# First norm scaled in the turn of the tokens, and its inputs loaded in another order

## The chip, the core and the metric

One core of a Trainium2 chip runs the whole kernel. The metric is device time in microseconds (us), lower is better. PE is TensorE, ACT ScalarE, DVE VectorE, POOL GpSimd, SP SyncE, which issues most of the DMA loads.

## What is computed

Two blocks one after the other on 256 tokens of 1024 channels in fp32. The change is in the first steps of the first block, for 16 meta tokens and the 256 of the input, T = 272 in all:

```python
h = jnp.concatenate([meta, x], axis=1)
u = rmsnorm(h, norm1_w[l])          # h * rsqrt(mean(h * h) + 1e-6) * norm1_w
proj = u @ w_in[l]
...
h = h + jnp.concatenate([out_a, out_b], axis=-1) @ w_out[l]
```

Behind it come the two mixers on `proj`, the output product, a gated MLP, and in the second block a modulation (`cond` times `w_ada`), retention, and a mixture of 16 experts whose weights (400 MB) are read from memory once.

## The kernel before

Every engine runs its own program, written out by hand; semaphores (`ev("name")`) order them. Activations lie with channels on the partitions: `hT` is the stream, `uT` the normed stream, each 8 tiles (KT) of 128 channels by 272 tokens. The inputs come with tokens on the partitions (`tok`, three windows of 128, 128 and 16 tokens), so they are turned first: PE's tile `x{k}` is made of three transposes (one a window, stationary operand a piece of `tok`, moving operand the identity), DVE copies it to `hT`. Tiles take turns in TB = 3 banks of PSUM in the order of the list `seq`; `open_tile` waits until the tile three before it is freed.

The start runs so. SP loads the constants `cst` (identity first, then masks and others, 1 MB), then the tokens in four loads; ACT issues ten small loads of parameter rows (`prow`, 124 rows). SP waits for all of these before it issues the first weights. PE waits for constants and tokens, turns x0 to x7 (L658), turns the parameter rows (L664, copied to `par` by DVE, L1587), and sums the squares with a matrix of 1/1024 (L649, tile n1); the squares are ACT's (L1274), written to `uT`. ACT takes the root of n1 (L1245), DVE its reciprocal over 128x272 (L1571), and scales each tile into `uT` (L1603): `hT` times norm1's weight times that reciprocal. PE's first projection tile p0 waits tile by tile for `uT` (`u_full`), and for its weights.

Weights stream through a ring of 2 MB units in the order of use (`stream(u)`, L502): u0 is the first block of `w_in`, for p0 to p3, u1 the first of `w_ada` (products L683, behind p3, which need `cond`), u2 the weights of p4 to p7, and so on. Behind u1 SP issues 20 more small loads (`more_parameters`), some of them of elements of 4 or 64 bytes. Projection tiles are L842, 8 products of 128x272 each; fp32 products are two instructions. ACT evicts tile p{j} (L1222); p0 to p11 feed DVE's convolution (`conv`, L1632, L1634), whose silu is ACT's (L1288). Other lines that are spoken of: L712 are transposes, L779 score products of 128x128, L1181 the experts' first products, L1093 later products of the second block.

Of the kernel before, what the change touches and what calls it, by code (L numbers as in the profile page):

```python
# [23 lines left out]
P = 128  # L24
D = 1024
# [123 lines left out]
def build(nc, a, out):  # L149
    with ExitStack() as ctx:  # L150
# [86 lines left out]
        chan = A.take(2, T)[0:16]  # L237

# [246 lines left out]
        def _(sp):  # L485
# [3 lines left out]
            load(cst[:], a["cst"], "cst_loaded")  # L489
# [107 lines left out]
        def _(pe):  # L597
# [213 lines left out]
            for j in range(NPROJ):  # L811
# [404 lines left out]
        def _(act):  # L1216
# [44 lines left out]
            rows("norm1", r1(a["norm1_w"]))  # L1261
            rows("lb0", r1(a["hg_lb_logits"][0:1]))
            rows("lb1", r1(a["hg_lb_logits"][1:2]))
            rows("hgn", r1(a["hg_norm_w"]))
            rows("m2cw", r1(a["m2_conv_w"][0]))
            rows("m2cb", r1(a["m2_conv_b"]))
            rows("m2n", r1(a["m2_norm_w"]))
            rows("norm2", r1(a["norm2_w"]))
# [6 lines left out]
            act.wait_ge(ev("par_ready"), 1)  # L1275
            act.wait_ge(ev("cond_cleared"), 1)
# [4 lines left out]
            act.wait_ge(ev("lb_shift"), 1)  # L1281
            act.activation(small[:, 0:16], small[:, 0:16], ACT.Exp).then_inc(ev("lb_exp"), 1)
            root("n1", T)
# [84 lines left out]
            for j in range(NPROJ):  # L1368
# [194 lines left out]
        def _(dve):  # L1563
# [16 lines left out]
            dve.memset(cond[:], 0.0).then_inc(ev("cond_cleared"), 1)  # L1580
            for k in range(KT):
                dve.wait_ge(ev("tiles_done"), k + 1)
                dve.tensor_copy(hT[:, k, :], bank_of(f"x{k}")[:, 0:T]).then_inc(ev("tiles_freed"), 1)
                dve.wait_ge(ev("tiles_freed"), k + 1)
                dve.nop().then_inc(ev("stream_tiles"), 1)
            dve.wait_ge(ev("par_turned"), 1)
            dve.tensor_copy(par[:, 0:PAR_ROWS[0]], ps[:, 3, 0:PAR_ROWS[0]]).then_inc(ev("par_ready"), 1)  # L1587
            dve.wait_ge(ev("par_ready"), 1)
# [4 lines left out]
            dve.nop().then_inc(ev("lb_shift"), 1)  # L1593
# [10 lines left out]

            inverse_root(T)
            for k in range(KT):
                scaled("norm1", k, 0)
# [16 lines left out]
            def conv(t):  # L1624
# [3 lines left out]
                if t == 0:  # L1628
                    dve.wait_ge(ev("tiles_done"), TN["n1"] + 1)
# [211 lines left out]
            for j in range(NPROJ):  # L1841
# [56 lines left out]
            for k in range(KT):  # L1898
                add_tile(f"o{k}", k, KEPT0)
                if 1 <= k < KT - 1:  # L1900
                    dve.wait_ge(ev("squares"), 2 * KT + k + 1)
# [325 lines left out]
```

## Time and profile before

| | |
|---|---|
| runs | 1725.61 us median of 3 (1721.76 to 1726.12) |
| the profiled execution | 1730.88 us, span 1729.1 us |
| PE busy | 1374.9 us, 80% of the span |
| DVE, ACT, POOL busy | 481.6, 409.9, 231.6 us |
| DMA | 523.98 MB, mean 303 GB/s; 430 GB/s in the second half |
| granted clock of PE, mean | 0.891 |
| chain that ended last | DMA 46%, PE 44%, DVE 7%, ACT 2% |

The profile is one execution with times from the span's start. Its rows name the engine, the line of the kernel, what is written and read, and how often. In groups the figures are busy us and mean ns of one instruction, then the engine's idle time before them and what ended it; in timelines and chains the start and the length in us; in windows of one engine the length, its busy time (instructions), the granted clock, the DMA share and GB/s. A granted clock of 1.00 is 2.4 GHz and 0.50 is 1.2 GHz.

### The profile page before, as it was taken

The numbers are of one execution on the slowest core, as the hardware profiler recorded it, in microseconds if no ns is written. First come the engines' busy times: TensorE is split into PE (matmuls) and PEld (weight loads), VectorE is DVE, ScalarE is ACT, GpSimd is POOL, SyncE is SP. The second block draws the span as 40 slices with busy tenths as digits, with TensorE's granted clock in tenths as the row PEclk, the third lists the DMA queues.
The fourth block names the chain that finished last, engine by engine and source line by source line (L and its number), as shares of the span: only waits on it lengthen the run. The fifth ranks groups of instructions, "written<-read, shape, count | busy, mean of one in ns | idle before, by whom it ended". The sixth has DMA issues, their size and how long they took to land.

```text
span 1729.1 us, 20537 instructions
## 1 busy us (share of the span) xinstructions
PE 1374.9 (80%) x8373; PEld 834.2 (48%) x8373; DVE 481.6 (28%) x901; ACT 409.9 (24%) x622; POOL 231.6 (13%) x100
## 2 busy tenths in 40 slices
PE   6999999999998999897776666667666666675665
PEld 4777788879998888854221222122212221221221
DVE  3443567626457365733000000000000000000001
ACT  3242356526664443612000000000000000000001
POOL 0000000027876754400000000000000000000000
PEclk9999999999999999996877887887888888888887
DMA  7843522139443563254999999999999999999995
GB/s 243 329 180 134 195 98 97 50 133 327 153 156 142 199 223 118 99 243 184 428 428 430 428 427 430 427 428 430 427 429 430 426 429 430 426 429 430 426 429 249
DMA packets 92189, 523.98 MB, mean 303 GB/s; under 512 B 7993, under 2 KB 30929, under 8 KB 64353
## 3 DMA queue, kind: packets, MB, share of 16 engines
q1 hardware_dynamic: 91913, 523.08, 74.4%
q8 instruction: 42, 0.69, 0.2%
q14 instruction: 18, 0.15, 0.0%
q10 hardware_dynamic: 216, 0.06, 0.0%
HBM read 522.08 MB, written 1.05 MB: 303 GB/s over the span
## 4 chain that ended last, share of the span: by engine, by line
DMA 46%; PE 44%; DVE 7%; ACT 2%; issue 1%; POOL 0%; SPq 0%; DVEq 0%; ACTq 0%
DMA ring<-in_w_up 23%; DMA ring<-in_w_down 23%; PE ps L842 9%; PE ps L634 5%; PE ps L638 5%; PE ps L635 5%; PE ps L1181 3%; PE ps L860 3%; PE ps L1194 3%; PE ps L1093 2%; PE ps L621 1%; PE ps L683 1%; PE ps L779 1%; DVE arena L1768 1%; DMA arena<-in_x 0%
## 5 line engine op out<-in xcount | busy, mean ns | idle before, releaser
L1181 PE MATMUL ps<-ring,arena 128*32 128x512 f32 x2000 | 299.2, 743 | 164.2 <-DMA ring<-in_w_up 138.5
L1559 POOL TENSOR_TENSOR ring_r<-ring,ring_r 128x1024 fp32r<-128x1024 f32 (+1 forms) x96 | 231.4, 2426 | 501.7 <-ACT ring_r L1233 500.9
L1194 PE MATMUL ps<-ring,arena 128*32 128x512 f32 x1024 | 175.2, 820 | 104.3 <-DMA ring<-in_w_down 97.5
L1181 PEld LDWEIGHTS ps<-ring,arena 128*32 128x32 f32 x2000 | 65.1, 126 | 381.5 <-DMA ring<-in_w_up 209.6
L634 PE MATMUL ps<-arena_r,ring_r 128*128 128x258 f32 (+2 forms) x752 | 226.9, 302 | 10.0 <-PE ps L638 3.0
L638 PE MATMUL ps<-arena_r,ring_r 128*128 128x258 f32 (+2 forms) x752 | 220.2, 293 | 0.0
L842 PE MATMUL ps<-uT,ring 128*128 128x272 f32 x832 | 203.7, 402 | 3.2 <-DVE uT L1603 3.2
L842 PEld LDWEIGHTS ps<-uT,ring 128*128 128x128 f32 x832 | 159.0, 194 | 38.8 <-issue 7.1
L634 PEld LDWEIGHTS ps<-arena_r,ring_r 128*128 128x128 f32 x752 | 143.0, 190 | 17.0 <-issue 9.3
L638 PEld LDWEIGHTS ps<-arena_r,ring_r 128*128 128x128 f32 x752 | 142.8, 190 | 2.8
L1194 PEld LDWEIGHTS ps<-ring,arena 128*32 128x32 f32 x1024 | 33.2, 131 | 227.7 <-DMA ring<-in_w_down 149.1
L2184 DVE TENSOR_TENSOR arena<-arena,ps 128x512 f32<-128x512 f32 x16 | 11.0, 687 | 449.5 <-PE ps L1181 449.5
L635 PE MATMUL ps<-arena_r,ring_r 128*128 128x256 f32 (+1 forms) x400 | 120.4, 301 | 0.0
L1233 ACT ACTIVATE ring_r<-ring 128x1024 fp32r<-128x1024 f32 (+1 forms) x96 | 98.7, 1033 | 27.5 <-PE ps L635 19.0
L635 PE MATMUL ps<-uT_r,ring_r 128*128 128x258 f32 x352 | 99.3, 282 | 0.0
L2186 DVE COPY arena<-ps 128x512 f32<-128x512 f32 x16 | 11.1, 691 | 294.2 <-PE ps L1194 294.2
L1531 ACT ACTIVATE arena<-ps 128x512 f32<-128x512 f32 x16 | 9.6, 597 | 318.4 <-PE ps L1186 318.4
L635 PEld LDWEIGHTS ps<-arena_r,ring_r 128*128 128x128 f32 x400 | 76.5, 191 | 3.7 <-issue 0.7
L1203 PE MATMUL ps<-arena 128*128 128x512 f32 x128 | 66.3, 666 | 14.2 <-DVEq L2193 13.4
L1529 ACT ACTIVATE arena<-ps 128x512 f32<-128x512 f32 x16 | 9.6, 597 | 282.1 <-PE ps L1181 282.1
L1535 ACT ACTIVATE arena<-ps 128x512 f32<-128x512 f32 x16 | 9.6, 597 | 268.9 <-PE ps L1194 268.9
L621 PEld LDWEIGHTS ps<-arena,hT 128*128 128x128 f32 x512 | 67.0, 208 | 8.9 <-issue 7.1
(365 smaller groups left out, 1436.2 us busy)
## 6 DMA issues: line engine op xcount, KB each, us to landing
ring<-in_w_gate SPq DMA_DIRECT2D x64, 2048.0 KB, 25.9
ring<-in_w_down SPq DMA_DIRECT2D x64, 2048.0 KB, 26.3
ring<-in_w_up SPq DMA_DIRECT2D x61, 2048.0 KB, 22.2
ring<-in_w_in SPq DMA_DIRECT2D x20, 2048.0 KB, 11.6
ring<-in_w_ada SPq DMA_DIRECT2D x12, 2048.0 KB, 8.0
ring<-in_ffn_w_up SPq DMA_DIRECT2D x22, 1024.0 KB, 8.0
ring<-in_w_out SPq DMA_DIRECT2D x6, 2048.0 KB, 9.2
ring<-in_ffn_w_down SPq DMA_DIRECT2D x4, 2048.0 KB, 8.7
```

The lines of the kernel that those rows point to most:

```text
L621: mm = pe.matmul(o, l, r, start=i == 0, stop=i == len(pairs) - 1)
L634: pe.matmul(o, hi[:, k, :], r_(xhi(k0 + k)), start=first and k == 0, stop=False)
L635: mm = pe.matmul(o, hi[:, k, :], r_(xlo(k0 + k)), start=False, stop=False)
L638: mm = pe.matmul(o, lo[:, k, :], r_(xhi(k0 + k)), start=False, stop=last and k == nk - 1)
L842: mm = pe.matmul(o[:, 0:T], w[:, k, :], uT[:, k, :], start=k == 0, stop=k == KT - 1)
L860: mm = pe.matmul(o[:, 0:KEPT], kcols(u_out[cb][half], m)[:, i, :], x, start=first and n == 0, stop=last and n == len(blocks) - 1)
L1093: mm = pe.matmul(ps[:, 4 + 2 * w + cb, :], x[:, w * P:w * P + P], slot(u_out2[cb]).rearrange("p (k c) -> p k c", k=KT)[:, i, :], start=n = ...
L1181: mm = pe.matmul(ps[32 * j:32 * j + 32, half, :], xs[:, kt, :], w[:, k, 512 * j:512 * j + 512], start=kt == 0, stop=kt == KT - 1)
L1194: mm = pe.matmul(ps[32 * j:32 * j + 32, half, :], heT[:, j, 32 * i:32 * i + 32], w[:, j, 512 * half:512 * half + 512], start=i == 0, stop= ...
L1203: mm = pe.matmul(ps[:, 4 + b, :], Gt[:, w * P:w * P + P], ye[:, half * 512:half * 512 + 512], start=first, stop=last, skip_group_check=True)
L1233: act.activation(r_(rounded(c)), chunks[c][1], ACT.Copy).then_inc(ev("w_hi"), 1)
L1559: pool.tensor_tensor(r_(w), w, f_(rounded(c)), ALU.subtract).then_inc(ev("w_lo"), 1)
```

## The change

1. SP loads only the identity (128 columns of `cst`) ahead of the tokens. The first weights u0 come directly behind the tokens, without the wait for the parameter rows; then seven rows of parameters that ACT issued before, then the rest of the constants, then u1. ACT keeps three small loads: norm1's row (with a semaphore of its own), c and cctx.
2. The mean square of each token is taken with tokens on the partitions: ACT squares windows 0 and 2 with a running sum (L1299), DVE window 1 (L1632, L1633); ACT takes three roots of one column each (L1301, L1311), DVE three reciprocals (L1638), and multiplies the identity's rows by them (L1639): `turned`, a diagonal matrix for each window.
3. New tiles `y{k}` (L690) are plain matmuls of `tok` with `turned`; DVE multiplies them by norm1's weight, a column, into `uT` (L1646). Tile n1, the squares, the root and the reciprocal over 272 columns are gone.
4. `hT` is still needed, for the residual: x0 to x4 are turned ahead of y0 to y7, x5 to x7 and the parameter rows behind p0. Their copies are ACT's now (L1306), and ACT evicts p0 between them. The silu and exp of small parameters on ACT, and what DVE makes of them, come behind x7's copy.

```diff
-        seq = [f"x{k}" for k in range(KT)] + ["n1"]
+        seq = [f"x{k}" for k in range(EARLY_X)] + [f"y{k}" for k in range(KT)]
         for j in range(NPROJ):
             seq += ["dt"] * (j == 12) + [f"p{j}"]
+            seq += [f"x{k}" for k in range(EARLY_X, KT)] * (j == 0)
...
-            load(cst[:], a["cst"], "cst_loaded")
+            load(cst[:, 0:P], a["cst"][:, 0:P], "ident_loaded")
...
             def stream(u):
-                if u == 0:
-                    sp.wait_ge(ev("par_loaded"), 16 * PAR_LOADS[0])
...
-            pe.wait_ge(ev("cst_loaded"), 16)
-            pe.wait_ge(ev("tok_loaded"), 64)
-            for k in range(KT):
+            def stream_tile(k):
...
-            pe.wait_ge(ev("par_loaded"), 16 * PAR_LOADS[0])
-            turn_parameters([0])
-            norm_sum("n1", T, lambda k: uT[:, k, :])
+            pe.wait_ge(ev("ident_loaded"), 16)
+            pe.wait_ge(ev("norm1_loaded"), 16)
+            pe.transpose(ps[:, 3, 0:8], prow[0:8, 0, :], ident[0:8, 0:8]).then_inc(ev("par_turned"), 1)
+            pe.wait_ge(ev("tok_loaded"), 64)
+            for k in range(EARLY_X):
+                stream_tile(k)
+            pe.wait_ge(ev("start_steps"), 5)
+            for k in range(KT):
+                o = open_tile(f"y{k}")
+                for w, (t0, n) in enumerate(WINDOWS):
+                    mm = pe.matmul(o[:, t0:t0 + n], tok[0:n, w, k * P:k * P + P], turned[0:n, w, 0:n], start=True, stop=True)
+                done(mm)
...
+                if j == 0:
+                    pe.wait_ge(ev("par_loaded"), 16 * (PAR_LOADS[0] - 1))
+                    pe.wait_ge(ev("start_steps"), 3)
+                    turn_parameters([0])
+                    for k in range(EARLY_X, KT):
+                        stream_tile(k)
+                    pe.wait_ge(ev("cst_loaded"), 16)
...
-            for k in range(KT):
-                act.wait_ge(ev("stream_tiles"), k + 1)
-                act.activation(uT[:, k, :], hT[:, k, :], ACT.Square).then_inc(ev("squares"), 1)
...
+            act.wait_ge(ev("tok_loaded"), 64)
+            for w in (0, 2):
+                n = WINDOWS[w][1]
+                st(act.activation(squares1[0:n, 0, :], tok[0:n, w, :], ACT.Square, accum_out=sums1[0:n, w:w + 1]))
+                st.wait()
+                act.activation(root1[0:n, w:w + 1], sums1[0:n, w:w + 1], ACT.Sqrt, scale=1.0 / D, bias=eps[0:n, 0:1]).then_inc(ev("root1"), 1)
...
+            st.link(tt(squares1[:, 1, :], tok[:, 1, :], tok[:, 1, :], ALU.mult))
+            st.link(dve.tensor_reduce(sums1[:, 1:2], squares1[:, 1, :], AX, ALU.add))
+            dve.nop().then_inc(ev("start_steps"), 1)
+            for i, w in enumerate((0, 2, 1)):
+                n = WINDOWS[w][1]
+                dve.wait_ge(ev("root1"), i + 1)
+                st.link(dve.reciprocal(inv1[0:n, w:w + 1], root1[0:n, w:w + 1]))
+                st(ts(turned[0:n, w, 0:n], ident[0:n, 0:n], inv1[0:n, w:w + 1], None, ALU.mult))
...
+                dve.wait_ge(ev("tiles_done"), TN[f"y{k}"] + 1)
+                ts(uT[:, k, :], bank_of(f"y{k}")[:, 0:T], norm1[:, k:k + 1], None, ALU.mult).then_inc(ev("tiles_freed"), 1)
...
-            inverse_root(T)
-            for k in range(KT):
-                scaled("norm1", k, 0)
```

SP's issues at the start, before (from its first):

```order
L487 DMA cst<-in_cst 128x2024
L487 DMA arena<-in_meta_tokens 16x1024
L487 DMA arena<-in_x 112x1024
L487 DMA arena<-in_x 128x1024
L487 DMA arena<-in_x 16x1024
L502 DMA ring<-in_w_in 128x8x512 [waits s_par_loaded]
L502 DMA ring<-in_w_ada 128x2x2048
L487 DMA arena<-in_final_norm_w 8x128
```

and now, from the third (the identity and the meta tokens stand ahead):

```order
L494 DMA arena<-in_x 112x1024
L494 DMA arena<-in_x 128x1024
L494 DMA arena<-in_x 16x1024
L507 DMA ring<-in_w_in 128x8x512
L494 DMA arena<-in_hg_lb_logits 8x128 x2
L494 DMA arena<-in_hg_norm_w 8x128
L494 DMA arena<-in_m_conv_w 48x128
L494 DMA arena<-in_m_conv_b 12x128
L494 DMA arena<-in_m_norm_w 8x128
L494 DMA arena<-in_norm_w 8x128
L494 DMA cst<-in_cst 128x1896
L507 DMA ring<-in_w_ada 128x2x2048
```

The first weights moved ahead of nothing but lost their wait; seven rows and the constants moved between them and the ada weights.

PE's rows at the end of the turns, before:

```order
L658 MATMUL ps<-cst,arena 128x128
L658 MATMUL ps<-cst,arena 128x16
L664 MATMUL ps<-cst,arena 128x124 [waits s_par_loaded]
L649 MATMUL ps<-uT,ones 128x272 [waits s_squares,s_tiles_freed]
L649 MATMUL ps<-uT,ones 128x272 [waits s_squares] x7
L842 MATMUL ps<-uT,ring 128x272 [waits s_u_full,s_slot0_loaded,s_tiles_freed]
```

and now, from the last of the y tiles on:

```order
L690 MATMUL ps<-arena 128x128 [waits s_tiles_freed]
L690 MATMUL ps<-arena 128x128
L690 MATMUL ps<-arena 128x16
L864 MATMUL ps<-uT,ring 128x272 [waits s_u_full,s_slot0_loaded,s_tiles_freed]
L864 MATMUL ps<-uT,ring 128x272 [waits s_u_full] x7
L677 MATMUL ps<-cst,arena 128x124 [waits s_start_steps,s_par_loaded]
L671 MATMUL ps<-cst,arena 128x128 [waits s_tiles_freed]
L671 MATMUL ps<-cst,arena 128x128
L671 MATMUL ps<-cst,arena 128x16
```

The sum of squares is out of PE's program; the parameter rows and x5 to x7 stand behind p0 (L864). In these rows a product counts once, whatever the number of its instructions.

## Rows read from the trace of the kernel before

**Rows 1.** The chain that ended last, 560 to 900 us: start, us, what
```profile
807.35 15.78 PE ps L1181 x128
...
832.47 26.48 DMA ring<-in_w_up
```

**Rows 2.** Who waited for whom, TensorE, 60 to 820 us: total, times, longest
```profile
PE ps L1106 <- DVE arena L2112: 4.0, 2, 3.2
```

**Rows 3.** The chain of the first 70 us
```profile
2.61 8.09 DMA arena<-in_x
...
10.83 6.71 PE ps L658 x24
...
17.94 6.02 PE ps L649 x16
...
24.61 1.86 DVE bc L1571
...
27.15 11.24 PE ps L842 x48
...
44.87 14.88 PE ps L842 x64
```

**Rows 4.** DMA view, 0 to 40 us in 40 slices of 1 us
```profile
GB/s 0 77 130 445 401 250 273 264 335 41 0 0 106 389 397 395 408 426 442 410 418 418 386 146 0 0 0 0 0 0 13 19 88 90 354 369 399 393 389 467
```

**Rows 5.** Timeline of SyncE's DMA issues: start, us
```profile
1.67 1.48 SPq L487 DMA_DIRECT2D arena<-in_x  x3
11.12 0.40 SPq L502 DMA_DIRECT2D ring<-in_w_in  x1
...
28.20 4.56 SPq L502 DMA_DIRECT2D ring<-in_w_in  x1
```

**Rows 6.** Instructions by line, ACT and DVE: busy us, mean ns | idle
```profile
L1515 ACT ACTIVATE arena<-arena 128x1024 f32<-128x1024 f32 x2 | 2.1, 1057 | 6.3 <-DVE arena L2112 6.3
...
L1222 ACT ACTIVATE arena<-ps 128x272 f32<-128x272 f32 x8 | 3.2, 397 | 28.0 <-PE ps L842 28.0
...
21.57 0.22 ACT L1282 ACTIVATE small<-small 128x16 f32<-128x16 f32 x1
...
L1783 DVE TENSOR_TENSOR arena<-arena 128x1024 f32<-128x1024 f32 x8 | 9.7, 1218 | 0.0
...
L2172 DVE COPY arena<-arena 128x128 f32 x30 | 5.4, 223 | 66.7 <-PE ps L1203 66.4 <-DVE arena L2164 0.2
```

**Rows 7.** TensorE's timeline near 203 and 222, windows with granted clock
```profile
202.71 2.97 PE L779 MATMUL ps<-arena 128*128 128x128 f32 x16
...
222.00 1.95 PE L779 MATMUL ps<-arena 128*128 128x128 f32 x16
...
204.00:205.00 1.00, 1.00 (x6) 0.50 1.06 408
...
207.00:208.00 1.00, 1.00 (x6) 1.00 1.06 389
```

**Rows 8.** Groups of TensorE's instructions, 20 to 22 and 22 to 24 us
```profile
L649 PE MATMUL ps<-uT,ones 128*128 128x272 f32 x6 | 2.9, 662 | 0.0
...
L649 PE MATMUL ps<-uT,ones 128*128 128x272 f32 x8 | 2.6, 476 | 0.0
```

**Rows 9.** DMA issues from 11 and from 28 us: KB, us to landing
```profile
ring<-in_w_in SPq DMA_DIRECT2D x1, 2048.0 KB, 7.7
...
ring<-in_w_in SPq DMA_DIRECT2D x1, 2048.0 KB, 13.1
```

**Rows 10.** Timeline of TensorE at 103 us and of DVE at 35 us
```profile
103.56 1.47 PE L712 MATMUL ps<-cst,arena 128*128 128x128 f32 x12
...
35.23 0.42 DVE L1632 TENSOR_SCALAR arena<-arena,par 128x272 f32<-128x272 f32 x1 [1.64 <-ACTq L1388]
```

**Rows 11.** Timeline of TensorE at 132 us
```profile
132.44 10.62 PE L842 MATMUL ps<-uT,ring 128*128 128x272 f32 x32
```

**Rows 12.** DMA queues, 0 to 2 us: packets, MB, share
```profile
q10 hardware_dynamic: 16, 0.00, 0.8%
```

More of the change, by code:

```diff
@@ L237, in build @@
         chan = A.take(2, T)[0:16]
+        at = A.at + 5 * T
+        turned = Arena(at).take(3, P)
+        norm1 = Arena(at + 3 * P).take(8)
+        sums1, root1, inv1 = (Arena(at + 3 * P + 8 + 4 * i).take(4) for i in range(3))
+        squares1 = Arena(at + 3 * P + 20).take(2, D)
+        EARLY_X = 5
         A = Arena(x_at)
@@ L537, in _ @@
                 stream(u)
+                if u == 0:
+                    rows("lb0", r1(a["hg_lb_logits"][0:1]))
+                    rows("lb1", r1(a["hg_lb_logits"][1:2]))
+                    rows("hgn", r1(a["hg_norm_w"]))
+                    rows("m2cw", r1(a["m2_conv_w"][0]))
+                    rows("m2cb", r1(a["m2_conv_b"]))
+                    rows("m2n", r1(a["m2_norm_w"]))
+                    rows("norm2", r1(a["norm2_w"]))
+                    load(cst[:, P:NCST], a["cst"][:, P:NCST], "cst_loaded")
                 if u == 1:
@@ L1259, in r1 @@
                 return w.rearrange("o (k p) -> (o k) p", p=P)
[L1261 to L1268, printed above, removed]
+            load(prow[0:8, 0, :], r1(a["norm1_w"].rearrange("(o d) -> o d", o=1)) if len(a["norm1_w"].shape) == 1 else r1(a["norm1_w"]), "norm1_loaded")
@@ L1269, in _ @@
             rows("c", r1(a["c_2"]))
             rows("cctx", a["c_ctx_2"].rearrange("(k p) -> k p", p=P))
-            for k in range(KT):
-                act.wait_ge(ev("stream_tiles"), k + 1)
-                act.activation(uT[:, k, :], hT[:, k, :], ACT.Square).then_inc(ev("squares"), 1)
-            act.wait_ge(ev("par_ready"), 1)
-            act.wait_ge(ev("cond_cleared"), 1)
+            act.wait_ge(ev("start_steps"), 1)
+            st(act.activation(root1[:, 3:4], eps[:, 0:1], ACT.Sqrt))
@@ new lines, in _, with stream_tile @@
+            act.wait_ge(ev("tok_loaded"), 64)
[4 more added lines that the diff above has]
+                act.activation(root1[0:n, w:w + 1], sums1[0:n, w:w + 1], ACT.Sqrt, scale=1.0 / D, bias=eps[0:n, 0:1]).then_inc(ev("root1"), 1)
+            def stream_tile(k):
+                act.wait_ge(ev("tiles_done"), TN[f"x{k}"] + 1)
+                act.wait_ge(ev("tiles_freed"), TN[f"x{k}"])
+                act.activation(hT[:, k, :], bank_of(f"x{k}")[:, 0:T], ACT.Copy).then_inc(ev("tiles_freed"), 1)
+                act.wait_ge(ev("tiles_freed"), TN[f"x{k}"] + 1)
+                act.nop().then_inc(ev("stream_tiles"), 1)
@@ new lines, in _ @@
+            act.wait_ge(ev("start_steps"), 4)
+            act.activation(root1[:, 1:2], sums1[:, 1:2], ACT.Sqrt, scale=1.0 / D, bias=eps[:, 0:1]).then_inc(ev("root1"), 1)
+            for k in range(EARLY_X):
+                stream_tile(k)
+            act.wait_ge(ev("tiles_freed"), TN["p0"])
+            evict("p0", proj[:, 4 * ORDER[0], :], T, ACT.Copy)
+            act.wait_ge(ev("tiles_freed"), TN["p0"] + 1)
+            act.nop().then_inc(ev("proj_tiles"), 1)
+            for k in range(EARLY_X, KT):
+                stream_tile(k)
@@ L1277, in _ @@
+            act.wait_ge(ev("start_steps"), 6)
+            act.wait_ge(ev("start_steps"), 2)
             st(act.activation(cond[:, :, 0], pc("c", 0, 8), ACT.Silu))
@@ L1279, in _ @@
             act.nop().then_inc(ev("cond_ready"), 1)
-            act.wait_ge(ev("lb_shift"), 1)
+            act.wait_ge(ev("start_steps"), 7)
             act.activation(small[:, 0:16], small[:, 0:16], ACT.Exp).then_inc(ev("lb_exp"), 1)
-            root("n1", T)
             def conv_silu(t):
@@ L1383, in _ @@
                     gate_squares(0)
+                if j == 0:
+                    continue
                 unit_ = ORDER[n]
@@ L1579, in _ @@
             st.wait()
-            dve.memset(cond[:], 0.0).then_inc(ev("cond_cleared"), 1)
-            for k in range(KT):
[L1582 to L1588, printed above, removed]
+            dve.nop().then_inc(ev("start_steps"), 1)
+            dve.memset(cond[:], 0.0).then_inc(ev("start_steps"), 1)
+            dve.wait_ge(ev("par_turned"), 1)
+            dve.tensor_copy(norm1, ps[:, 3, 0:8]).then_inc(ev("start_steps"), 1)
+            dve.wait_ge(ev("tok_loaded"), 64)
+            st.link(tt(squares1[:, 1, :], tok[:, 1, :], tok[:, 1, :], ALU.mult))
+            st.link(dve.tensor_reduce(sums1[:, 1:2], squares1[:, 1, :], AX, ALU.add))
+            dve.nop().then_inc(ev("start_steps"), 1)
+            for i, w in enumerate((0, 2, 1)):
[3 more added lines that the diff above has]
+                st(ts(turned[0:n, w, 0:n], ident[0:n, 0:n], inv1[0:n, w:w + 1], None, ALU.mult))
+            st.wait()
+            dve.nop().then_inc(ev("start_steps"), 1)
+            dve.wait_ge(ev("start_steps"), 3)
+            dve.wait_ge(ev("tiles_freed"), EARLY_X)
+            for k in range(KT):
+                dve.wait_ge(ev("tiles_done"), TN[f"y{k}"] + 1)
+                ts(uT[:, k, :], bank_of(f"y{k}")[:, 0:T], norm1[:, k:k + 1], None, ALU.mult).then_inc(ev("tiles_freed"), 1)
+                dve.wait_ge(ev("tiles_freed"), TN[f"y{k}"] + 1)
+                dve.nop().then_inc(ev("u_full"), 1)
+            dve.wait_ge(ev("par_turned"), 2)
+            dve.tensor_copy(par[:, 0:PAR_ROWS[0]], ps[:, 3, 0:PAR_ROWS[0]]).then_inc(ev("start_steps"), 1)
+            dve.wait_ge(ev("start_steps"), 6)
             st.link(tt(small[:, 16:24], pc("lb0", 0, 8), pc("lb1", 0, 8), ALU.max))
@@ L1628, in conv @@
                 if t == 0:
[L1629 removed]
+                    dve.wait_ge(ev("tiles_done"), TN["x7"] + 1)
+                    dve.wait_ge(ev("cst_loaded"), 16)
                 if t >= 2:
@@ L1900, in _ @@
                 if 1 <= k < KT - 1:
-                    dve.wait_ge(ev("squares"), 2 * KT + k + 1)
+                    dve.wait_ge(ev("squares"), KT + k + 1)
                     ins = tt(uT[:, 0, 0:KEPT], uT[:, 0, 0:KEPT], uT[:, k, 0:KEPT], ALU.add)
@@ L1976, in _ @@
                 if 1 <= k < KT - 1:
-                    dve.wait_ge(ev("squares"), 3 * KT + 2 * k + 2)
+                    dve.wait_ge(ev("squares"), 2 * KT + 2 * k + 2)
                     st(tt(hx[:, 0, 0:L], hx[:, 0, 0:L], hx[:, k, 0:L], ALU.add))
```

4 lines of the change are left out of this document (2 added, 2 removed).

## The prediction

> **What bounds the kernel now.** I read the chain that ended last first. Up to some 825 us it is TensorE's work with short waits; from 832 us on it is expert weights arriving, 26 us at a time [rows 1]. All TensorE's waits from 60 to 820 us are small, the largest group 4.0 us [rows 2]. The expert loads begin when TensorE gives ring slots back, so a microsecond won ahead of the first projection moves the whole rest, DMA part included. The second reading is the start itself: tokens awaited until 10.70, 24 transposes of 6.71, the sum of squares of 6.02, root, a reciprocal of 1.86, scaling, and the first projection tile p0 at 27.15; p4 at 44.87 follows the ada products with no wait [rows 3]. p1 then starts at 30.9 (27.15 + 16 x 0.234, with 0.234 = 11.24 / 48). The third reading is what ends the wait for tokens: the slices of 1 us of DMA traffic show 1.05 MB in slices 1 to 4 (the constants), then 1.16 MB in slices 5 to 9 (the tokens, slower), then nothing until 12 [rows 4], since SyncE holds the first weights back to 11.12 [rows 5].
>
> **The tokens land earlier.** Of the constants' 1.036 MB only 0.066 MB stay ahead of the tokens. The 0.97 MB that go behind cost, at slices 3 and 4 (423 GB/s) [rows 4], 2.3 us: last landing 10.70 - 2.3 = 8.4. That is my value, the nearest row. Lower bound: if the tokens are slow (273 GB/s) only because of the small rows that ACT issued beside them (216 packets on its queue; seven of its ten loads move away), they take 2.75 us instead of 4.2, and land at 7.0. Upper bound: 9.1, the 128 narrow rows of the identity costing more than their bytes. Below 5.1 it can't go: the last token load is issued at 3.15 and a lone small load needs about 2 us.
>
> **From tokens T to p0.** PE turns x0 to x2 at 0.84 a tile (6.71 / 8) [rows 3], until T + 2.6. x3 needs a free bank, and the copies are now ACT's, which first does two squares (1.06 for one of 128x1024) and three roots (a little over 0.2 each with its wait, as the exp of 16 columns took 0.22): free at T + 2.9, first copy 0.40 [rows 6], x3 from T + 3.4, x4 done at T + 5.1. This stall of 0.8 is new. Beside it, and hidden: DVE's 1024-wide product and sum, at most 2 x 1.22 [rows 6], then three reciprocals and three scalings of at most 128x128, some 0.2 each (a copy of that size took 0.223), of which only the last pair follows ACT's last root, ready at T + 3.5 [rows 6]. If PE's x tiles were quicker, this chain would be next at T + 3.5.
> The y tiles are ordinary fp32 matmuls, two instructions for each product, so 48 for eight tiles. Price of one: the 16 of L779 at 222.00, 128x128 fp32 too, took 1.95, 0.12 each; the 16 at 202.71 took 2.97, of which the last ten or so ran at a granted 0.50, that is 1.2 GHz, at some 0.22 each [rows 7]. Which level rules here? The clock column reads 1.00 all through the start, but the sum's matmuls of 128x272 took 662 ns until 22 and 476 on average from 22 to 24 [rows 8], and p0's ran at 0.234 apart against 0.45 for 272 columns twice at 1.2 GHz: the lower level, 1.2 GHz, until about 22.5, 11.7 us after the first transpose and 4.8 us after the first ordinary matmul. So I count 4.8 us at 0.22 (22 instructions) and 26 x 0.12 = 3.1: y takes 7.9. Bounds: full clock from the start 5.8, none 10.6. DVE scales a tile in about 0.44 beside 0.72 of PE, and hides. The weights of p0 are issued at 3.2 instead of 11.12 and landed 7.7 after issue [rows 5, 9]; landed by 14, as the tokens' last byte is followed by 2.1 MB at 0.4 MB/us, they are early. p0 starts at T + 5.1 + 7.9 = 21.4.
> The Trainium skill (Perfetto Trace Analysis, Transposes) speaks against this edit: it wants logical transposes done in transpose mode and not as a plain matmul. The trace agrees on the count, two instructions for one; by it the eight y tiles would be 24 instructions, 2.9 at full clock, and the edit throws some 3 us away against that; the sum above stands without it.
>
> **After p0.** p0 runs 3.75 as before. Behind it now stand the 124-row transpose of parameters and x5 to x7, ten transposes; twelve such at full clock took 1.47 [rows 10], so 1.2, and 1.35 with ACT's two copies of 0.40 that free p1's bank. The seven parameter rows and the other constants (behind p0's weights, 1 MB, done by about 17) are long there. p1 starts at 21.4 + 3.75 + 1.35 = 26.5 against 30.9: **4.4 us earlier**. The sum of squares (6.02), the root, the wide reciprocal and the scaling of 8 tiles in one piece (3.2 of idle PE) are gone; y, the late transposes and the stall take much of it back. ACT's two table loads and the silu and exp of the small parameters come after x7's copy now, about 3.4 us; DVE's first convolution starts some 4 us later in its tile, but before each convolution DVE idles 1.64 in a tile of 3.7 [rows 10], so three tiles absorb it, and three banks keep PE going. Cost nothing.
>
> **What is late next.** The weights of p4 are issued at 28.20 and land 13.1 later, 41.3 [rows 5, 9]; p4 began at 44.87. Now p4 is wanted at 40.5. SyncE's queue takes seven row loads and one of constants more ahead of the ada weights (some 0.4 of issue each, 3.3 in all), yet issues those at 7 instead of 11.57, and the rest moves up with them: the pause of 2.8 us in the traffic (9.3 to 12.1) closes and the first data starts as before, the bytes are the same, so these weights should land at 38.5. It holds by 2.0 us.
>
> **Sum.** The profiled execution took 1730.88 (span 1729.1); minus 4.4 is 1726.5. It stands 5.3 above the median of the runs, 1725.61, so the median I expect is 1721.2.
>
> **The rivals.**
> (a) Forecast, 1721.2; own range 1719.5 to 1723. Chance 0.50.
> (b) The tokens come at full rate, T = 7.0: 1.4 more, 1719.8. For it: the same slices give 273 against 423 GB/s with engines busy. Against: 216 packets of 512 B are little work. 0.17.
> (c) Slower: the diagonal products don't wake the clock. Place: PE from y0. The point that decides is whether y raises the clock before p0. If it counts as little as the transposes did, y runs at their 0.278 (0.84 / 3) for 48 = 13.3 (+5.4), p0 at 2 x 0.227 x 16 = 7.25 (+3.5), the ten transposes at 0.278 (+1.45): 10.3 lost, 5.9 slower, 1731.5. The Trainium skill (TensorE: Matmul & The Clock Gate, Part 4) says that transposes don't release the clock; the trace agrees (nothing rose in 6.7 us of them), and the rule leaves plain matmuls out of it. Against the rival: the granted clock fell to 0.50 at 204 and was back at 1.00 by 207, while PE ran just such 128-wide products [rows 7]. 0.06.
> (d) The clock rises, but later: at 132.44 thirty-two matmuls took 10.62 instead of 7.5 [rows 11], so some 14 of them, 6.4 us, ran at 1.2 GHz, though they were dense. Then y costs 8.7 and the gain is 3.6: 1722.0. 0.12.
> (e) p4 waits for its weights. From u1's last byte (23) to p4's weights there are 18 us of tiny loads; if that tail doesn't move, p4 starts at 41.4: 0.9 lost, 1722.1; if the seven rows and the constants ahead stretch it by 3, 1724. 0.08.
> (f) The change doesn't bring the tokens forward (the slow tokens are bound by something else, or PE waits for the norm1 row, which stands ahead of them in its program). Without the 2.3: 1723.5. Against: ACT's queue moved its first 16 packets before 2.0 us [rows 12]. 0.07.
>
> **How the numbers follow.** About 0.3% (5.2 us) is what a measurement of this kernel can tell from no change; three runs of before lie 4.4 apart. (b) alone passes 5.2, 0.13 of its 0.17; in (a) 4.4 is short of it by less than the scatter of a median, so 0.19 of its 0.50; 0.03 from the rest: faster 0.35. Slower: 0.04 of (c) and 0.01 of scatter. The rest, 0.60, is within. The range takes in (b) and (f) with the 4.4 of the three runs beyond each: 1715.5 to 1728; outside are (c) and the far ends.
>
> **What would show it.** In the profile after: last token landing at 8.4; x0 to x2 at 0.83 a tile, a wait of PE on ACT before x3; y tiles 1.3 us apart first and 0.72 later, with a step after about 4 tiles; p0 at 21.4, p1 at 26.5, p4 at 40.5 without a DMA wait. Wrong if p1 isn't 3 to 6 us earlier, or if what is won at p1 isn't found again at the first expert load.

## The result and the profile after

| | before | changed |
|---|---|---|
| median of 12 runs each | 1724.46 us (1721.57 to 1726.12) | 1726.97 us (1725.54 to 1731.17) |
| ratio to before, 95% interval | | 1.0019, 1.0010 to 1.0027 |
| the profiled execution, span | 1730.88, 1729.1 | 1730.58, 1728.8 |

The change makes the kernel slower by 0.19%, some 3.3 us by the ratio of the runs (the medians lie 2.5 apart), where 4.4 us less were forecast. It is less than 0.3%, but clear of the scatter and on the other side.

TensorE's timeline of the changed kernel, start and length in us, answers to [rows 3]:

```profile
8.63 2.57 PE L671 MATMUL ps<-cst,arena 128*128 128x128 f32 x9 [5.69 <-DMA arena<-in_x]
11.97 1.74 PE L671 MATMUL ps<-cst,arena 128*128 128x128 f32 x6 [0.77 <-ACT hT L1306]
13.63 13.56 PE L690 MATMUL ps<-arena 128*128 128x128 f32 x48
27.12 5.53 PE L864 MATMUL ps<-uT,ring 128*128 128x272 f32 x16
...
34.14 7.60 PE L864 MATMUL ps<-uT,ring 128*128 128x272 f32 x32
...
46.30 1.92 PE L705 MATMUL ps<-ring,cond 128*32 128x512 f32 x16 [0.30 <-PE ps L864]
```

Up to y0 it is the forecast: tokens in time for x0 at 8.63 (forecast 8.4), the wait on ACT ahead of x3, y0 at 13.63 (13.5). Then the 48 instructions of the y tiles take 13.5 us where 7.9 were expected, and p0 takes 5.4 instead of 3.75. p1 starts at 34.1 and not at 26.5; before it was 30.9. So 3.2 us are lost at p1, and p4, behind the ada products at 46.30, starts 3.35 later than before (48.22 against 44.87 [rows 3]), with no wait for its weights.

The y tiles by form, PE and then its weight loads, 13.6 to 27 us (busy us, mean ns | idle):

```profile
L690 PE MATMUL ps<-arena 128*128 128x128 f32 x32 | 9.8, 461 | 0.0
L690 PE MATMUL ps<-arena 16*128 16x16 f32 x16 | 4.8, 380 | 0.0
```

```profile
L690 PEld LDWEIGHTS ps<-arena 128*128 128x128 f32 x32 | 7.4, 322 | 0.3
```

and p0's at its start and its end (27.2 to 30.2, then 30.8 to 32.4):

```profile
L864 PE MATMUL ps<-uT,ring 128*128 128x272 f32 x7 | 3.5, 674 | 0.0
```

```profile
L864 PE MATMUL ps<-uT,ring 128*128 128x272 f32 x9 | 2.2, 392 | 0.0
```

A weight load of 322 ns and a matmul of 128x272 of 674 ns are the figures of the lower level, as the sum's 662 were [rows 8]; 392 is full clock. PE ran at 1.2 GHz all through x, y and half of p0, and the clock came only some 3.5 us into p0's wide products. PE was never waiting meanwhile: it was busy for all of the 13.5 us. DVE was not the limit either; from the third y tile on it idled 1.19 us ahead of each scaling, as here:

```profile
18.80 0.50 DVE L1646 TENSOR_SCALAR uT<-ps,arena 128x272 f32<-128x272 f32 x1 [1.19 <-PE ps L690]
```

The two profiled executions hide the loss: 1730.58 is as long as 1730.88. From p4 to the first long wait for expert weights the one of before took 787.6 us (44.87 to 832.47 [rows 1, 3]), that of the change 784.7 (48.22 to 832.96). Two falls of the clock account for it. At the first, the 32 products near 132 took 10.62 us in before [rows 11] and 9.29 in the changed kernel, where TensorE's windows show a shorter fall:

```profile
136.00:137.00 1.00, 1.00 (x4) 0.60 0.97 356
137.00:138.00 1.00, 1.00 (x3) 0.50 0.13 45
...
139.00:140.00 1.00, 1.00 (x4) 0.69 0.00 0
```

(stretch, length, busy us and instructions, granted clock, DMA share, GB/s.) At the second, the clock of before fell behind a wait of 1.86 us on GpSimd that ended at 564.8:

```profile
566.00:568.00 2.00, 2.00 (x12) 0.50 0.97 407
```

In the changed kernel it had fallen ahead of that wait, from 556.0 to 559.5, and there it cost nothing: both kernels then had to wait for GpSimd, until 564.80 and 566.54. The lead of before is 3.05 us ahead of the first fall and 1.7 behind it, still 1.7 at the end of that wait, and 0.3 behind the second fall. Such falls differ between two executions of one kernel: in scaled_warm, below, the granted clock was at 0.50 for 3.4 us near 170 and again near 194, in best_again, the same kernel, for 6.8 us near 170 and not near 194. The part behind differs too: from the first long wait for expert weights to the end of the span it is 892.4 to 896.7 us in the fourteen traces, whatever the start was. So p1 in one trace gives the time only to within some 4 us, and the medians, not this pair, carry the verdict.

### The profile page after: what moved, and what is told of

Same layout as the page of the kernel before. It is cut to its first block, busy times and chain, and to the rows that moved or that the text cites. A ratio compares the mean times of both kernels' runs of the same rounds, so it can differ in the third digit from the quotient of the medians.

```text
span 1728.8 us, 20632 instructions
## 1 busy us (share of the span) xinstructions
PE 1382.7 (80%) x8406; PEld 839.7 (49%) x8406; DVE 480.6 (28%) x901; ACT 410.9 (24%) x628; POOL 231.3 (13%) x100
## 4 chain that ended last, share of the span: by engine, by line
DMA 46%; PE 44%; DVE 6%; ACT 2%; issue 1%; SPq 0%; POOL 0%; DVEq 0%; ACTq 0%
DMA ring<-in_w_up 23%; DMA ring<-in_w_down 23%; PE ps L864 9%; PE ps L648 5%; PE ps L652 5%; PE ps L649 5%; PE ps L1210 3%; PE ps L889 3%; PE ps L1223 3%; PE ps L1122 2%; PE ps L635 1%; PE ps L705 1%; PE ps L801 1%; PE ps L690 1%; DVE arena L1828 1%
## 5 line engine op out<-in xcount | busy, mean ns | idle before, releaser
L864 PE MATMUL ps<-uT,ring 128*128 128x272 f32 x832 | 204.2, 402 | 0.0
L864 PEld LDWEIGHTS ps<-uT,ring 128*128 128x128 f32 x832 | 158.8, 194 | 35.4 <-issue 3.4
L1232 PE MATMUL ps<-arena 128*128 128x512 f32 x128 | 65.3, 657 | 14.2 <-DVEq L2253 13.5
```

The lines of the kernel that those rows point to most:

```text
L864: mm = pe.matmul(o[:, 0:T], w[:, k, :], uT[:, k, :], start=k == 0, stop=k == KT - 1)
L1232: mm = pe.matmul(ps[:, 4 + b, :], Gt[:, w * P:w * P + P], ye[:, half * 512:half * 512 + 512], start=first, stop=last, skip_group_check=True)
```

## The experiments

Theory C: the granted clock is the cause. PE runs the x and y tiles and half of p0 at 1.2 GHz, since nothing in the y tiles raises it. Its rival, theory S: the diagonal products are slow by their structure, two instructions for each of their 24 products and a third of them on 16 rows, at either clock. Beside both stands the question which of the change's two parts costs.

Every ratio is to before, run on the same chip.

| kernel | median us | before, same chip | 95% interval of the ratio | y tiles us | p0 us | p1 starts |
|---|---|---|---|---|---|---|
| changed | 1726.97 | 1724.46 | 1.0010 to 1.0027 | 13.5 | 5.4 | 34.1 |
| loads_only | 1723.84 | 1725.86 | 0.9975 to 0.9996 | - | - | - |
| norm_only | 1729.76 | 1725.86 | 1.0011 to 1.0032 | 13.5 | 5.7 | 36.9 |
| warm | 1719.84 | 1725.86 | 0.9947 to 0.9972 | 7.7 | 3.8 | 26.5 |
| scaled_turn | 1720.54 | 1725.86 | 0.9952 to 0.9979 | 6.7 | 6.6 | 28.6 |
| y_filled | 1728.24 | 1724.71 | 1.0017 to 1.0037 | 17.4 | 3.7 | 35.4 |
| warm_short | 1726.20 | 1724.71 | 0.9995 to 1.0015 | 13.5 | 6.2 | 34.7 |
| scaled_warm | 1717.19 | 1724.71 | 0.9948 to 0.9972 | 4.6 | 3.8 | 23.9 |
| loads_warm | 1723.94 | 1724.71 | 0.9990 to 1.0007 | - | - | - |
| y_no_small | 1716.89 | 1725.08 | 0.9941 to 0.9969 | 6.3 | 3.7 | 25.1 |
| loads_gap | 1719.52 | 1725.08 | 0.9963 to 0.9981 | - | - | - |
| best_again | 1717.82 | 1725.08 | 0.9948 to 0.9974 | 4.5 | 3.8 | 23.3 |
| y_grouped | 1718.27 | 1725.46 | 0.9948 to 0.9975 | 6.2 + 2.0 | 5.3 | 28.9 |

The y and p0 columns are from y0's first instruction to p0's first, and on to the one behind p0 (a gap behind the y tiles counts with neither). The kernels on before's norm have no y tiles.

### The two parts apart: loads_only and norm_only

loads_only is before with the change's order of loads:

```diff
-            load(cst[:], a["cst"], "cst_loaded")
+            load(cst[:, 0:P], a["cst"][:, 0:P], "ident_loaded")
...
-                if u == 0:
-                    sp.wait_ge(ev("par_loaded"), 16 * PAR_LOADS[0])
```

(and the seven rows and the other constants behind u0, as in the change). norm_only is the change with before's loads ahead of the tokens.

> The kernel before with the new order of loads alone (identity, tokens, first weights, seven rows, other constants), norm as it was. In the changed kernel the tokens landed at 8.6 us instead of 10.7. If that gain is real and nothing else uses it up, everything from the first transpose on moves up by 2.1 us: p1 at 28.8 instead of 30.9, and the time is 2.1 us under before. A rival, that the order of loads is itself what costs (p4's weights late, or p0's), gives no gain or a loss here. Both theories of the slow y tiles give the same here.

> The changed kernel's norm, late x tiles and late rows, with the loads of before (all constants ahead of the tokens, first weights held back for the rows). If the two parts add, tokens at about 10.7 and p1 2.1 us later than in the changed kernel, at 36.3, which is 5.4 us over before.

TensorE's timeline in loads_only:

```profile
8.26 6.71 PE L665 MATMUL ps<-cst,arena 128*128 128x128 f32 x24 [8.26 <-DMA arena<-in_x]
...
15.15 5.17 PE L656 MATMUL ps<-uT,ones 128*128 128x272 f32 x16
23.69 12.93 PE L849 MATMUL ps<-uT,ring 128*128 128x272 f32 x48 [3.37 <-DVE uT L1605]
```

The order of loads is worth what was forecast: tokens 2.6 us earlier, time 0.15% less (interval 0.04 to 0.25%). The rival that it costs is out. But p0 to p2 take 12.93 instead of 11.24 [rows 3], which the granted clock explains: PE waited from 20.3 to 23.7 for root and reciprocal, and 1.0 us behind that wait, at 24.7, the clock fell, until 28.1:

```profile
24.00:25.00 1.00, 1.00 (x5) 0.83 0.05 0
...
26.00:27.00 1.00, 1.00 (x4) 0.50 0.35 28
...
28.00:29.00 1.00, 1.00 (x6) 0.96 0.62 55
```

In norm_only p1 starts at 36.9, 6.0 us behind before and 2.8 behind the change, so in the trace the parts add. The time, 1.0022, is 3.8 us over before and not 5.4; 5.4 is just within the interval (1.9 to 5.5). So the norm, as written, is what costs, and the loads gave part of it back.

### Is it the clock? warm and warm_short

PE has nothing to do from 2.9 to 8.6. In warm it does eight products of 128x512 of the `ones` matrix there, into a bank that nobody reads:

```diff
+            def fill(n):
+                for _ in range(n):
+                    pe.matmul(ps[:, 7, :], ones[:], ones[:].unsqueeze(1).to_broadcast([P, 4, P]), start=True, stop=True)
+
+            pe.wait_ge(ev("start_steps"), 1)
+            fill(2)
             pe.wait_ge(ev("ident_loaded"), 16)
...
+            fill(6)
             pe.wait_ge(ev("tok_loaded"), 64)
```

> The changed kernel, and PE does eight products of 128x512 of the ones matrix, which nobody reads, while it waits for the tokens (2 ahead of the norm1 row's turn, 6 behind it), to raise the clock first. Theory C (the y tiles are slow because PE ran at 1.2 GHz all through them and they did not raise the clock): if the clock then stays up, x tiles take 0.36 instead of 0.84, y tiles 0.72 instead of 1.69, p0 3.75 instead of 5.5, and p1 starts about 9.5 us earlier than in the changed kernel, at 24.6: 6 us under before. If it falls again while PE turns x0 to x4 and waits for ACT, y is as slow as now. Theory S (a y instruction takes 0.28 by itself, by its weight loads and the change between pieces of 128 and 16 rows): y stays at 1.69 a tile whatever the clock, and only p0 gains, 1.7 us.

```profile
1.45 3.78 PE L682 MATMUL ps<-ones 128*128 128x512 f32 x4 [1.45 <-DVEq L1634]
...
5.36 5.63 PE L682 MATMUL ps<-ones 128*128 128x512 f32 x12
...
13.42 7.76 PE L697 MATMUL ps<-arena 128*128 128x128 f32 x48
21.11 3.93 PE L871 MATMUL ps<-uT,ring 128*128 128x272 f32 x16
```

Theory C holds. The first four idle instructions are 0.93 apart, the last twelve 0.46: the clock rises near 5.4. The y tiles take 7.7 us (the prediction's 7.9), 0.16 an instruction instead of 0.28, and p0 3.8. The tokens had landed at 7.7, where DVE's square of them starts, and ACT's first copy waits for PE's x0:

```profile
7.71 1.23 DVE L1639 TENSOR_TENSOR arena<-arena 128x1024 f32<-128x1024 f32 x1 [2.08 <-DMA arena<-in_x]
```

```profile
11.40 0.40 ACT L1313 ACTIVATE hT<-ps 128x272 f32<-128x272 f32 x1 [0.67 <-PE ps L671]
```

So the idle products, which end at 10.8, run 3.1 us past the tokens, and it is they that set y0 at 13.42: here ACT waits for PE, and in the changed kernel PE waited for ACT. By the steps of the changed kernel (x3 0.3 behind ACT's last root, which ended at 10.74, then six transposes in 1.0) it could have started near 12.1, an estimate. p1 is 7.6 us earlier than in the change, and the time falls to 0.996. The forecast had p1 1.9 earlier still, at 24.6, as it counted 0.72 for a y tile and it took 0.96. Theory S keeps a small part: at full clock a y instruction takes 0.16 and not L779's 0.12 [rows 7].

warm_short has `fill(3)` in place of `fill(6)`.

> As warm, with 5 idle products instead of 8, so that they end near 8.4, as the tokens land, instead of 10.8. The clock is up at 8.4. ACT's squares and copies bound x3 and y0, so y0 starts at 13.0 to 13.4 as in warm. If the clock holds through the x tiles and their wait, as it did with the dense work up to 10.8, the time is that of warm or 0.4 better; if it falls in between, y is slow for part of its length and the time lies 1 to 6 us over warm.

```profile
5.00 2.84 PE L682 MATMUL ps<-ones 128*128 128x512 f32 x6
8.34 1.66 PE L671 MATMUL ps<-cst,arena 128*128 128x128 f32 x9 [0.49 <-DMA arena<-in_x]
11.67 1.74 PE L671 MATMUL ps<-cst,arena 128*128 128x128 f32 x6 [1.68 <-ACT hT L1313]
13.34 13.56 PE L697 MATMUL ps<-arena 128*128 128x128 f32 x48
```

```profile
10.00:11.00 1.00, 0.00 (x0) 1.00 1.06 391
12.00:13.00 1.00, 1.00 (x5) 0.50 1.16 373
...
26.00:27.00 1.00, 1.00 (x5) 0.50 0.38 32
```

The idle products end at 7.8, the x tiles start at full clock (1.66 for nine instead of 2.57), but PE then waits 1.7 us for ACT, and at about 11.3 the granted clock goes to 0.50, that is 1.2 GHz. It stays there until 31.7, through all y tiles, which are just as long as in the changed kernel. Here the column itself shows the level that in the changed kernel had to be read from durations (it says 1.00 there throughout). This is the direct sight of the mechanism: 13.5 us of unbroken y products did not bring the clock back. The runs are of two kinds, three of twelve at 1718.85 to 1722.45 and nine at 1726.1 to 1726.8, as if the clock held through the wait in some; only the one execution has a trace, so this is a reading and not shown.

### What in the y tiles keeps the clock down: y_filled, y_no_small, y_grouped

y_filled puts one idle product of 128x512 behind each y tile (the same `pe.matmul` as above, behind `done(mm)`).

> The changed kernel with one product of 128x512 of the ones matrix, which nobody reads, behind each y tile (two instructions, 0.85 us at 1.2 GHz, 0.43 at 2.4). y0 starts as now, at low clock. Theory C, that the y tiles did not raise the clock by being what they are, and dense work does: the clock rises some 4 to 7 us behind y0, tile pitch goes from 2.5 to about 1.4 within the y tiles, p0 comes at 27 to 29 in spite of 16 instructions more, and runs at full clock (3.75 instead of 5.5); in all within 2 us of the changed kernel. Rival, that the clock rises at a moment of its own whatever PE does: pitch 2.5 to the end, p0 at 34, 5 us over the changed kernel.

```profile
16.28 1.60 PE L690 MATMUL ps<-arena 128*128 128x128 f32 x6
17.81 1.57 PE L692 MATMUL ps<-ones 128*128 128x512 f32 x2
19.21 0.93 PE L690 MATMUL ps<-arena 128*128 128x128 f32 x6
20.07 1.12 PE L692 MATMUL ps<-ones 128*128 128x512 f32 x2
...
30.13 3.83 PE L865 MATMUL ps<-uT,ring 128*128 128x272 f32 x16
```

The clock rises near 18, within the second idle product, 5 us behind y0; from then on six y instructions take 0.86 instead of 1.69, and p0 comes at full clock. The rival of a moment that PE's work doesn't touch is out: with the same y tiles the clock rises in 5 us with wide work among them, and not in 13.5 without. The pitch of 1.82 behind it is longer than forecast, so p1 is 1.3 us later than in the change, though the tokens came 0.9 sooner (7.7).

y_no_small drops the y products of the third window. It leaves part of the computation out: the last 16 tokens aren't normed.

```diff
-                for w, (t0, n) in enumerate(WINDOWS):
+                for w, (t0, n) in enumerate(WINDOWS[0:2]):
                     mm = pe.matmul(o[:, t0:t0 + n], tok[0:n, w, k * P:k * P + P], turned[0:n, w, 0:n], start=True, stop=True)
```

> The changed kernel without the y products of the third window (the last 16 tokens are not normed: that part of the computation is left out), so 32 instructions of 128x128 back to back instead of 48 with every third pair on 16 rows. The scores L779 of before, of just this shape back to back, stood 0.22 apart at 1.2 GHz and the clock rose behind them. If it is the pieces of 16 rows that thin out PE's work, the pitch of a tile is 0.9 instead of 1.13 (4 x 0.28) and the clock rises within the y tiles, 3.5 to 7 us behind y0: y takes 6 to 7, p0 3.75, 8 us under the changed kernel's start of p1. If products against a diagonal don't raise the clock whatever their density, pitch 0.9 or 1.13 to the end, y 7 to 9, and p0 5.5 again: 5 to 6 us under.

```profile
13.48 6.48 PE L690 MATMUL ps<-arena 128*128 128x128 f32 x32
19.80 3.83 PE L864 MATMUL ps<-uT,ring 128*128 128x272 f32 x16
```

```profile
18.16 0.50 DVE L1646 TENSOR_SCALAR uT<-ps,arena 128x272 f32<-128x272 f32 x1 [0.35 <-PE ps L690]
19.01 0.50 DVE L1646 TENSOR_SCALAR uT<-ps,arena 128x272 f32<-128x272 f32 x1 [0.35 <-PE ps L690]
19.66 0.50 DVE L1646 TENSOR_SCALAR uT<-ps,arena 128x272 f32<-128x272 f32 x1
```

DVE's scalings show the tiles' pitch: 0.85 (four instructions at 0.21, as L779 at the lower level) up to 19, then 0.65, which is DVE's own pace as it no longer waits. 32 instructions stood in 6.3 us, p0 took 3.67 from its first to the transposes, and p1 started 9.0 us ahead of the change's, where 8 were expected. So the clock rises in the y tiles when the pieces of 16 rows are gone, about 5.5 us behind y0. Each of these pieces costs twice, by itself and by an idle gap of the weight loads, as PE's weight loads in the changed kernel show: the first gap (0.23), and the group of all 16, whose loads take 308 ns each, nearly the 322 of a full piece:

```profile
14.78 0.28 PEld L690 LDWEIGHTS ps<-arena 16*128 16x128 f32 x1 [0.23 <-issue]
```

```profile
L690 PEld LDWEIGHTS ps<-arena 16*128 16x128 f32 x16 | 4.0, 308 | 1.8 <-issue 1.8
```

With 0.85 for the four instructions on 128 rows, as in y_no_small, the two on 16 rows take the other 0.84 of a tile's pitch of 1.69. What it is in these pieces that holds the clock down, their few rows or the gaps at their loads, no run here separates.

y_grouped is the whole kernel again: the same eight small products, in one run behind y7.

```diff
-                for w, (t0, n) in enumerate(WINDOWS):
+                for w, (t0, n) in enumerate(WINDOWS[0:2]):
                     mm = pe.matmul(o[:, t0:t0 + n], tok[0:n, w, k * P:k * P + P], turned[0:n, w, 0:n], start=True, stop=True)
                 done(mm)
+            for k in range(KT):
+                mm = pe.matmul(ps[:, 5, 16 * k:16 * k + 16], tok[0:16, 2, k * P:k * P + P], turned[0:16, 2, 0:16], start=True, stop=True)
+            mm.then_inc(ev("y_last"), 1)
```

> The changed kernel, whole, but the y products of the third window (16 rows each) are taken out of the tiles and made in one run of eight behind y7, into a bank of their own, and one DVE instruction scales them. If the pieces of 16 rows were what kept the clock down, it rises in the y tiles as in y_no_small: y0 to y7 in 6.3, the eight small products in 16 x 0.16 = 2.6 or less at full clock, 0.4 for DVE, p0 at about 22.9 and in 3.75, p1 at 28.1 against 34.1 in the changed kernel: 6 us under it and 3 under before. If something else than their place matters, as their number, y stays at 13.5 and p0 comes at 27.

```profile
13.24 6.26 PE L690 MATMUL ps<-arena 128*128 128x128 f32 x32
19.43 1.95 PE L693 MATMUL ps<-arena 16*128 16x16 f32 x16
21.99 5.48 PE L867 MATMUL ps<-uT,ring 128*128 128x272 f32 x16 [0.60 <-DVEq L1654]
```

```profile
21.00:22.00 1.00, 0.40 (x5) 0.88 0.21 36
22.00:23.00 1.00, 1.00 (x2) 0.50 0.05 0
...
25.00:26.00 1.00, 1.00 (x6) 0.91 0.38 30
```

The same products in another order: y0 to y7 in 6.2 us and the small ones in 1.95, 8.2 where they took 13.5. The place of the small pieces is what mattered, not their number. Behind them the clock fell, at 21.8, only 0.4 us into the wait of 0.6, so this execution's p0 took 5.3 and p1 started at 28.9, not 28.1. Whether that short wait or the 1.95 us of 16-row products ahead of it let the clock fall is not separated. The time, by its ratio of 0.9962, is 6.6 us under before, more than p1's 2.0 would give. The traces say where more can come from: the first long wait for expert weights begins 4.5 us ahead of before's (827.92 against 832.47), since near 132 the granted clock was low for 3.4 us here and for 6.8 in before, and behind that point y_grouped took 892.4 us and before 896.6. Both differ from one execution to the next, so for the medians the split stays open; at 1722.1 the profiled execution was also the slowest of five, and the other four lie between 1717.9 and 1719.1.

### Other ways: scaled_turn, scaled_warm, loads_warm, loads_gap

scaled_turn scales the tokens and turns them in transpose mode:

```diff
-                st(ts(turned[0:n, w, 0:n], ident[0:n, 0:n], inv1[0:n, w:w + 1], None, ALU.mult))
+                st(ts(tokn[0:n, w, :], tok[0:n, w, :], inv1[0:n, w:w + 1], None, ALU.mult))
...
-                    mm = pe.matmul(o[:, t0:t0 + n], tok[0:n, w, k * P:k * P + P], turned[0:n, w, 0:n], start=True, stop=True)
+                    mm = pe.transpose(o[:, t0:t0 + n], tokn[0:n, w, k * P:k * P + P], ident[0:n, 0:n])
```

> The changed kernel, but DVE multiplies the tokens themselves by the inverse root (a column, 128x1024 for each window, 0.85 us each) and PE turns the scaled tokens in transpose mode against the plain identity: 24 instructions instead of 48. y starts at about T + 5.4 and takes 8 x 0.84 = 6.7 instead of 13.6; p0, still at the lower clock at first, 5.5 to 7. p1 starts 5 to 6.5 us earlier than in the changed kernel, 2 to 3 us under before. Theory S gives the same, as it counts instructions; C too, unless the clock rises at another time.

24 instructions took 6.7 us, and p0 6.6, all but its last us at the lower clock; p1 starts at 28.6, 5.5 us earlier than in the change and 2.3 earlier than in before. The time, by its ratio of 0.9966, is 5.9 under before; in this trace the clock did not fall near 132 at all, so part of the difference can again lie there. The plain matmuls cost twice the instructions, and here, at the lower clock, that is 6.8 us, not the 3 that the prediction took from rows at full clock. The Trainium skill (Perfetto Trace Analysis, Transposes) asks for the transpose mode; the trace agrees, 6.7 us against 13.5. The Trainium skill (TensorE: Matmul & The Clock Gate, Part 4) says too that transposes don't release the clock; the trace agrees, as scaled_turn's stood 0.28 us apart to the last and p0 came at the lower clock.

> scaled_turn with warm's 8 idle products. x tiles until 13.4, tokens scaled at about 13.9, the y turns at DVE's pace of 0.85 to 0.95 a tile, p0 at about 20.5 against 21.1 in warm and 20.4 in scaled_turn. If the clock holds through 7 us of transposes, p0 takes 3.75 and the time is 0.5 under warm; if transposes let it fall, p0 takes 5 to 7 and it is 1 to 3 over warm.

> scaled_warm again, for a narrower interval and beside loads_gap on one chip: 0.996 of before, 6.5 to 7.5 us under it; in its profile p0 at 18.5 and p1 at 23.9.

```profile
11.30 2.66 PE L672 MATMUL ps<-cst,arena 128*128 128x128 f32 x15
13.89 4.55 PE L698 MATMUL ps<-cst,arena 128*128 128x128 f32 x24
18.48 3.93 PE L872 MATMUL ps<-uT,ring 128*128 128x272 f32 x16
```

The timeline is scaled_warm's. It has the earliest p1 of the whole kernels and the lowest median, 7.5 us under before, and 7.3 when it was measured again as best_again, 0.996 both. By the ratio it is not told apart from warm (0.9960) or y_grouped (0.9962). The y turns took 4.6 us, 0.57 a tile, where 0.85 to 0.95 was forecast. Here too the idle products set the start: they ended at 11.30 in scaled_warm and at 10.54 in best_again, and y0 started at 13.89 and 13.37. 39 transposes in a row, 7 us, did not let the raised clock fall, though the same ones did not raise it in scaled_turn.

loads_gap puts three of the idle products behind the sum in loads_only; loads_warm puts five ahead of its tokens.

> loads_only with three idle products of 128x512 behind the sum n1, in the gap of 3.4 us in which PE waits for root and reciprocal. In loads_only's profile the clock fell 4.5 us behind the sum's end and three of p0's tiles cost 1.7 us more. With the gap filled the clock holds: p0 to p2 in 11.24 as in before, time 0 to 1.7 us under loads_only (by how often it fell), 2.5 to 4 under before. A rival, that the gap has no part in it, gives loads_only's time.

> The norm as before, the new order of loads, and 5 idle products ahead of the tokens. Tokens at 8.3; transposes at DVE's pace of the copies, 0.6 a tile instead of 0.83; n1's sum 3.75 instead of 5.2 to 6; then the gap of 3.3 for root and reciprocal. p0 at 20.5 to 21.5 against 23.7 in loads_only, no x tiles left behind p0, p1 at 24.5 to 25 if the clock holds over the gap: 1.5 us under warm. If it falls in the gap, p0 takes 1.7 more and it equals warm. This tells whether the new norm is worth anything once the clock is up.

In loads_gap p0 to p2 took 11.24 and the ratio was 0.9972 where loads_only's was 0.9985; the intervals overlap, so the gap's cost is seen in the trace and only likely in the time. In loads_warm the x tiles were quick, 4.28 for the eight, and nothing came of it. PE stood until 14.7 for the parameter rows, which the new order puts behind 2 MB of weights, and the clock fell in that wait. Behind the gap at the sum it was low again, 0.50 at 25 to 26. The waits of 0 to 30 us (us, count, longest) and the window of the first fall:

```profile
PE ps L852 <- DVE uT L1609: 3.2, 1, 3.2
PE ps L674 <- DMA arena<-in_norm_w: 2.2, 1, 2.2
```

```profile
14.00:15.00 1.00, 0.26 (x2) 0.50 0.94 351
```

So its forecast was wrong by a wait that wasn't counted, and whether the old norm could match the new one with the clock up is not settled by it.

## Why the prediction was wrong

- **What bounds the kernel:** right in kind. What p1 loses or wins arrives at the first expert load, but for the falls of the clock in between, which in single traces are as large as the change: from p1 to that load before took 801.6 us, the change 798.8, and scaled_turn 797.2.
- **Tokens earlier:** right, 8.6 for 8.4, and in loads_only 8.3. The tokens still came at 260 to 330 GB/s with seven of ACT's ten loads gone, so rival (b) is out.
- **From T to y0:** right, T + 5.0 for 5.1, with the stall of 0.8 on ACT.
- **The y tiles:** the step that failed, "I count 4.8 us at 0.22 (22 instructions) and 26 x 0.12 = 3.1: y takes 7.9". Both halves were off. An instruction takes 0.28 at the lower clock and not 0.22, with every third product on 16 rows; and the clock never rose. It was rival (c), at 0.06: its 13.3 for y was met by 13.5; p0 took 5.4 and not 7.25, as the clock rose 3.5 us into it; the ten transposes took 1.6 and not 2.8. By (c) 5.9 slower, measured 3.3. The three misses, 5.6 at y, 1.6 at p0 and 0.3 at the transposes, make up, but for 0.1, the way from 4.4 earlier at p1 to 3.2 later.
- **Why (c) was priced so low:** against it stood the rise near 207 with 128-wide products on PE [rows 7]. Those were of one shape back to back, 0.22 apart. y_no_small has just that form and the clock rises; the change's y tiles have not. The forecast took two things for the same by their operand shape and did not work out the pitch of a whole tile at the lower clock, though the transposes, with the same weights and the same 16-row pieces, showed 0.28 [rows 3].
- **After p0, p4's weights:** right for the weights, issued at 25.49 and landed 10.5 later, at 36.0 (forecast 38.5); p4 itself came at 48.2, so rival (e) was put to no test in this kernel, but in best_again p4 started at 37.4 without a wait for them. By its own terms, 0.9 and 3 on 1721.2, (e)'s second figure is 1725.1 and not 1724. Ten transposes and the parameter rows 1.6 for 1.35 (32.5 to 34.1), the late small work on ACT and DVE delayed nothing, p4 had its weights.
- **The saving of the norm itself:** as it was written, none at the lower clock, where the longer y tiles take more than the sum, the root and the gap behind them gave. At full clock it is not shown: the 6 us by which warm is under before are the loads, the raised clock and the norm together. The old norm with the new loads and its gap filled has p1 at 27.6 (loads_gap, 23.84 and 3.75) against warm's 26.5, its x tiles at the lower clock, and the ratios, 0.9972 and 0.9960, have intervals that overlap.

## What to carry to other kernels

At the start of a kernel like this one price TensorE's work at 1.2 GHz until something wide has run, and ask of each new stage whether it would raise the clock. In this kernel products 272 and 512 wide did so 1.8 to 5.6 us behind the first of them (1.8 in loads_gap's sum, 3.9 in warm's idle products, 5.6 in scaled_turn's p0), 128-wide ones on full rows after 5.1 and 5.5, and the same with a 16-row piece in every third place not in 13.5, in three traces. Where PE waits for the first data anyway, idle products there cost little, about 1.3 us in warm by the estimate above, for what they run past the data. But they have to leave no long wait behind them: with three fewer, ended 3 us earlier, the clock fell in the traced run and the median was that of before. Keep odd small pieces together instead of one in each tile, and fold a per-token factor into the tokens ahead of a transpose sooner than into a diagonal matrix.

## What the runs showed of the hardware that was not expected

- The granted clock column can read 1.00 at the start of a program while PE runs at half of it: 674 ns against 392 for one shape. Once the clock has been up, the column follows (0.50 in warm_short).
- The length of a gap of PE did not tell whether the clock fell. It fell 0.4 us into a wait of 0.6 in y_grouped, behind small products, and 0.5 us into one of 2.2 in loads_warm; it fell 1.0 us behind the end of one of 3.4 in loads_only, and held over 3.2 in the profiled execution of before [rows 3]. At the wait on GpSimd near 565 it fell behind 1.86 in before and 1.82 in norm_only, and held over 1.84 in warm_short and 1.83 in loads_only, where it had fallen some 12 us ahead of the wait's end.
- The weight load of a 16-row piece took 308 ns at the lower clock, nearly as long as that of a full one, 322.
- A row of parameters issued behind 2 MB of weights on the same queue made PE wait until 14.7 us (loads_warm).
